# A head's sum of squares in the hgrn mixer: two rounded products instead of one plain F32 product

## What is computed

```python
proj = einsum('bsd,de->bse', h, w_in)
q, f_logit, i_val, g = split(proj, ...)
f = lb + (1.0 - lb) * sigmoid(f_logit)          # one decay for each token and key column
k = 1.0 - f
# in chunks of 64 tokens, 8 heads of 128 columns, state [128 keys, 128 values]:
o = (q * exp(b)) @ state + scores(q, k, b) @ v   # b: running sum of log f within the chunk
state = exp(b_last)[..., None] * state + (k * exp(b_last - b)).T @ v
...
o = rmsnorm(o, g_norm_w) * silu(g)               # over the 128 columns of each head
return einsum('bsd,de->bse', o, w_out)

def rmsnorm(x, g):
    return x * rsqrt(mean(x * x, axis=-1) + EPS) * g
```

## Time and profile before

| what | value |
|---|---|
| median of three runs | 2321.96 us (2321.89 to 2322.27) |
| profiled execution, span | 2320.9 us |
| instructions | 32131 |
| granted TensorE clock over the span | 1.000 |
| DMA, mean over the span | 98 GB/s, 226.30 MB |
| the hgrn head loop and its end | about 690 to 845 us of the span |
| TensorE busy in that stretch | 152.22 of 155.00 us |
| VectorE, ScalarE, GpSimd busy in it | 126.50, 130.46, 61.95 us |

### The profile page before, as it was taken

One profiled execution on the slowest core, in us unless ns is written; L12 is line 12 of the kernel. 1 busy time (PEld: TensorE's weight loads), 2 busy tenths in 40 slices (PEclk: granted clock), 3 DMA queues, 4 the chain that ended last, 5 costly groups with the idle time before them and its releaser, 6 DMA issues.

```text
span 2320.9 us, 32131 instructions
## 1 busy us (share of the span) xinstructions
PE 2309.1 (99%) x12088; PEld 1950.9 (84%) x12088; DVE 1498.3 (65%) x2173; ACT 1119.0 (48%) x1829; POOL 223.6 (10%) x313
## 2 busy tenths in 40 slices
PE   9999999999999999999999999999999999999999
PEld 8777889988888888999888778888888878888887
DVE  6665789952738968899428876777434456777731
ACT  6655544452539965445326854444323444544420
POOL 1221013200125410232000000000001000000000
PEclk9999999999999999999999999999999999999999
DMA  5433223332242222333322223323322323233232
GB/s 167 152 132 102 85 92 109 104 112 93 87 118 64 64 84 82 99 110 111 113 89 77 64 82 91 100 90 106 100 93 91 100 69 95 91 100 100 95 107 79
DMA packets 72541, 226.30 MB, mean 98 GB/s; under 512 B 7921, under 2 KB 19489, under 8 KB 72417
## 3 DMA queue, kind: packets, MB, share of 16 engines
q1 hardware_dynamic: 67840, 210.72, 28.5%
q0 software_dynamic: 4576, 13.89, 1.9%
HBM read 221.28 MB, written 2.18 MB: 96 GB/s over the span
## 4 chain that ended last, share of the span: by engine, by line
PE 92%; DVE 3%; ACT 3%; POOL 1%; issue 1%; DMA 0%; DVEq 0%; ACTq 0%; SPq 0%
PE bank L338 26%; PE bank L340 25%; PE bank L339 25%; PE bank L478 5%; PE bank L470 4%; PE bank L1605 1%; PE bank L1596 1%; PE bank L1639 1%; DVE w_lo L312 0%; DVE h L756 0%; POOL hgrn_lv L2560 0%; PE bank L2651 0%; PE bank L2015 0%; POOL hgrn_lv L2547 0%; PE bank L3103 0%
## 5 line engine op out<-in xcount | busy, mean ns | idle before, releaser
L312 DVE TENSOR_TENSOR w_lo<-raw,w_hi 128x1024 fp32r<-128x1024 f32 (+1 forms) x310 | 402.3, 1308 | 218.4 <-ACT w_hi L307 218.1
L338 PE MATMUL bank<-x_hi,w_hi 128*128 128x512 f32 x1344 | 529.2, 394 | 1.2 <-ACT sb_q L2761 1.0
L340 PE MATMUL bank<-x_hi,w_lo 128*128 128x512 f32 x1344 | 523.4, 389 | 0.0
L339 PE MATMUL bank<-x_lo,w_hi 128*128 128x512 f32 x1344 | 523.1, 389 | 0.0
L307 ACT ACTIVATE w_hi<-raw 128x1024 fp32r<-128x1024 f32 (+1 forms) x310 | 344.6, 1121 | 179.9 <-PE bank L340 93.5
L338 PEld LDWEIGHTS bank<-x_hi,w_hi 128*128 128x128 f32 x1344 | 252.3, 188 | 57.4 <-issue 3.1
L340 PEld LDWEIGHTS bank<-x_hi,w_lo 128*128 128x128 f32 x1344 | 252.2, 188 | 53.0
L339 PEld LDWEIGHTS bank<-x_lo,w_hi 128*128 128x128 f32 x1344 | 252.5, 188 | 51.2 <-issue 0.5
L338 PE MATMUL bank<-st_a_hi,w_hi 128*128 128x512 f32 (+1 forms) x396 | 145.1, 366 | 0.0
L340 PE MATMUL bank<-st_a_hi,w_lo 128*128 128x512 f32 (+1 forms) x396 | 144.7, 365 | 0.0
L1374 DVE TENSOR_TENSOR bank<-bank,rstd 128x512 f32<-128x512 f32 x120 | 83.2, 696 | 92.2 <-PE bank L340 92.2
(11 more groups left out here) (444 smaller groups left out, 4673.2 us busy)
## 6 DMA issues: line engine op xcount, KB each, us to landing
raw<-in_w_up SPq DMA_DIRECT2D x120, 512.0 KB, 3.5
raw<-in_w_down SPq DMA_DIRECT2D x64, 704.0 KB, 4.2
st_raw_even<-in_w_up SPq DMA_DIRECT2D x28, 512.0 KB, 4.2
st_raw_odd<-in_w_up SPq DMA_DIRECT2D x24, 512.0 KB, 4.0
raw<-in_w_fox_qk SPq DMA_DIRECT2D x16, 512.0 KB, 3.7
raw<-in_w_hgrn_qf SPq DMA_DIRECT2D x16, 512.0 KB, 3.5
fox_c_keys_a<-fox_c_rows POOLq DMA_DIRECT2D x8, 640.0 KB, 4.1
fox_c_keys_b<-fox_c_rows POOLq DMA_DIRECT2D x8, 640.0 KB, 4.5
```

The lines of the kernel that those rows point to most:

```text
L312: nc.vector.tensor_tensor(w_lo[:, slot, 0:size], raw[:, slot % 2, 0:size], w_hi[:, slot, 0:size].bitcast(F32), ALU.subtract).then_inc(sem( ...
L338: nc.tensor.matmul(out, w[0], x[0], start=first, stop=False)
L339: nc.tensor.matmul(out, w[0], x[1], start=False, stop=False)
L340: return nc.tensor.matmul(out, w[1], x[0], start=False, stop=last)
```

## The change

ScalarE squares bank 7 twice: into `ho` as plain F32, and into a new tile `square_hi` rounded to F32R. VectorE subtracts, `square_low = ho - square_hi`, also F32R (`square_rest`). TensorE multiplies both by rounded ones (`ones_r`) and adds them up in bank 5. `norm` waits for both squares ahead of the high product and for the subtraction ahead of the low one. `square_low` lies at the address of `ho`, so the subtraction is in place, and `square_hi` lies at the address of `hr`. `square_rest` stands between product 0 and product 1 in the loop, ahead of `near_take` in turn 8 and ahead of the weight conversion in turns 9 and 10. `hg_square_low` takes over the semaphore `fx_qk`.

```diff
-            "gla_min": ("fx_setup", 4), "gla_abs": ("fx_ls", 3),
+            "gla_min": ("fx_setup", 4), "gla_abs": ("fx_ls", 3), "hg_square_low": ("fx_qk", FOX_PAIRS),
...
         hg_masks_at = hg.at
+        at_ho = hg.at
         ho, hr = (hg.take(n, [P, T])[:] for n in ("ho", "hr"))
+        square_low, square_hi = (hg.take(n, [P, T], F32R, at=at_ho + 4 * T * i)[:] for i, n in enumerate(("square_low", "square_hi")))
...
             def norm(o):
 
-                wait(pe, "hg_sq", o + 1)
+                wait(pe, "hg_sq", 2 * o + 2)
                 wait(pe, "hg_st", 3 * o + 3)
-                nc.tensor.matmul(ps[5][:], ones[:], ho, start=True, stop=True).then_inc(sem("hg_ms"), 1)
+                nc.tensor.matmul(ps[5][:], ones_r[:], square_hi, start=True, stop=False)
+                wait(pe, "hg_square_low", o + 1)
+                nc.tensor.matmul(ps[5][:], ones_r[:], square_low, start=False, stop=True).then_inc(sem("hg_ms"), 1)
...
                         nc.scalar.activation(ho, ps[7][:], ACT.Square).then_inc(sem("hg_sq"), 1)
+                        nc.scalar.activation(square_hi, ps[7][:], ACT.Square).then_inc(sem("hg_sq"), 1)
...
+                def square_rest():
+                    if norm:
+                        wait(dve, "hg_sq", 2 * o + 2)
+                        tt_(square_low, ho, square_hi.bitcast(F32), ALU.subtract, "hg_square_low")
+
...
                 if proj:
                     product(0)
+                    square_rest()
                     product(1)
...
                 elif lev:
+                    square_rest()
                     near_take()
...
                 else:
+                    square_rest()
                     second_unit()
                     near_take()
```

## The result

The changed kernel takes 2325.89 us (median of 20 runs, 2324.93 to 2327.00) against 2322.31 us for the kernel before on the same chips (20 runs, 2321.53 to 2325.49): a ratio of 1.0015, interval 1.0009 to 1.0021, or +3.6 us (2.1 to 4.9). That lies inside the 0.2% that I had called no change, and on its slower side. The forecast was +2.2 us. The profiled execution happens to be the fastest of the 20. It spends 1.8 us outside its span, so its 2324.93 us are 2323.1 us of span, and that of before, 2320.9 us of span, stands for some 2322.7. (The 1.1 us named ahead of the prediction were the distance of that span from the median of three runs, and not the launch's ends, which are 1.8 us.) This pair alone shows +2.2 us, by luck the forecast; where the other 1.4 us come from had to be found out.

The account below looks back on a forecast made before the run. TensorE, 99% busy, was taken to set the pace, with ScalarE and VectorE close behind; 0.3 + 0.3 + 0.65 + 0.95 + 0 = +2.2 us, from 2321.96 to 2324.2 us, range 2321.0 to 2326.8 us.

Parts of the forecast that it names:

- TensorE saves 0.41 us a head: At each head's norm, two rounded products take 0.45 us in place of 0.86: 3.3 us less for eight heads.
- ScalarE +0.49 us, 0.15 left at kd: In the loop the second square costs ScalarE 0.49 us; waits cover part, leaving kd 0.15 us late, with 0.17 to spare.
- Low product, stall 0.24, pair 0.16 us earlier: In mid-loop TensorE stalls 0.24 us for the subtraction, so the pair gains 0.16 us in place of 0.41.
- State products wait for kd in every turn: In the loop kd is later by 0.15 us, so state products wait for ScalarE and start only 0.02 us earlier.
- Heads 2 to 4, +0.3: Mid-loop turns lose 0.10 us each, 0.12 for contention less 0.02 gained: +0.3 us (-0.15 to +1.4).
- the GpSimd rival: Subtraction's 0.60 us step delays GpSimd's level 2 difference, then kd: 0.43 us a head, total 2326.3 to 2328 us; 14%.
- Heads 0 and 1, +0.3: Early turns, where TensorE already waits, lose by ScalarE's 0.15 us lateness: together +0.3 us (0 to +0.9).
- Head 5, +0.65: At the tail the subtraction stands behind a weight conversion; TensorE stalls 1.5 us, VectorE wins back 0.45: +0.65 us (0.2 to 1.1).
- Head 6, +0.95: At the tail the subtraction comes after the takes, the pair ends at 830.42 against 829.46: +0.95 us (0.5 to 1.4).
- Head 7, 0: At the last head the low product waits about as long as the pair saves: 0 us (-0.4 to +0.3).
- Nothing behind the mixer takes it up: Behind the mixer TensorE has no gap to absorb the loss, so the +2.2 us goes to the end.
- the milder reading: VectorE's subtraction beside GpSimd: 0.12 us taken for contention, near the milder row, 0.61 us against 0.41; worst case 1.26.

Follow-up runs that it names:

- the second profile: The changed kernel as it is, profiled once more: 2326.19 us, with a span of 2324.4 us.
- the first: First profile of the changed kernel, the fastest of its 20 runs: 2324.93 us, with a span of 2323.1 us.
- the four profiles with a fallen clock: Variants of the changed kernel: pair in heads 0 to 4 only, 2323.58 us; subtraction earlier at the tail, 2325.82; norm later in the loop, 2326.48; both orders, 2325.43.

## Why the prediction was right, and where it was off

The direction, the class and the range (2321.0 to 2326.8) hold: 2325.89 us. Of the mechanism the larger half holds: TensorE's saving doesn't reach the end, and the tail is lost to a subtraction that stands behind other VectorE work. In mid-loop it holds for kd without the subtraction, but not with it: three of the signs that I gave didn't come (low product 0.4 to 0.6 us after the high one, near earlier, state products waiting for kd), and what the turn loses there it loses by the subtraction and GpSimd, which I had priced at 0.12 us. The size was 2.2 us for 3.6 measured. By its steps:

- **TensorE saves 0.41 us a head.** Confirmed where nothing waits: without the subtraction the pair takes 0.46 us from start to start instead of 0.86. By the page the busy time fell by 1.2 us only: with a stall in between, the page counts 0.40 us for the high product and 0.34 for the low one up to the next start, 0.74 against 0.86.
- **ScalarE +0.49 us, 0.15 left at kd.** Measured 0.49 and 0.11.
- **Low product, stall 0.24, pair 0.16 us earlier.** Wrong: counted as I did, from start to start, the stall is 0.71 - 0.23 = 0.48 us, twice the forecast (the bracket's 0.31 leaves out 0.17), and near starts 0.19 us later. The 0.12 us for contention was too little: the subtraction took 0.89 us, 0.21 more than 0.68, just what the row in its own place had shown (0.61 against 0.41 us), and GpSimd's difference grew by 0.27. Nor did I price that the matmul after the stalled one comes 0.34 instead of 0.23 us later.
- **State products wait for kd in every turn.** True without the low product's wait, not with it, where TensorE itself arrives later than kd.
- **Heads 2 to 4, +0.3.** Measured +0.60 and +0.49. It was the GpSimd rival in small: level 2 starts 0.27 to 0.29 us later against its turn, just short of the 0.3 from which I said it decides. The turn, 17.40 us in the second profile and 17.44 in the first, stands at the upper edge of the 17.1 to 17.4 that I gave, or just over it.
- **Heads 0 and 1, +0.3.** -0.05 with the race won, +0.61 with it lost, and in the four profiles with a fallen clock 0.2 to 0.5 us more (34.65 to 34.93 us from head 0's state products to head 2's, against 34.45). The term was sized from one profiled execution, and of the terms inside the mixer it is the one that varies most.
- **Head 5, +0.65.** Measured +1.0. The stall was right (1.58 us for 1.5), the 0.45 us to be won back weren't: the product did fall from 1.26 to 0.41 us, but VectorE waits 0.60 us for ScalarE's exponential (819.47), and ScalarE had waited 0.84 us for the turn of kd (818.32), which stands behind TensorE's stall. The second square, for which I had nothing at the tail, costs 0.6 us there by itself. **Head 6, +0.95:** 1.10. **Head 7, 0:** 0.1.
- **Nothing behind the mixer takes it up.** In both profiles 0.4 us are taken back at the norm that follows the mixer. In starts, TensorE is 2.53 us behind ahead of it; its wait for sum_lo, 0.5 us before, is gone, which leaves 1.77; and the wait for x_hi, 0.8 instead of 0.4, makes it 2.12. That the change is the cause isn't shown: the kernel with the plain product at the tail takes back 0.6 us at the same place.

The sum of these is +3.0 us for the second profile, in which the clock stayed at 1.00; with the 0.2 to 0.5 us of a fallen clock it is 3.2 to 3.5 of the 3.6 us measured, and the rest is within the interval. How often the clock falls in the 20 runs is not known. What stays open, too, is why some executions enter the mixer later than others, before any instruction that was changed: from 0.3 us earlier to 2.4 us later than the profile of before.

## What to carry to other kernels

A shorter list for the busiest engine is worth little when the chain that feeds it is as long: here kd, through ScalarE and GpSimd, was 0.2 us from being awaited. Take the work that the change gives them, not the work it takes from TensorE, as the first term. A wait that appears in front of the new instruction is not yet its cost; remove it and look whether the turn gets shorter, and if the next wait takes its place, the chain behind both is what to shorten. The cost also hangs on where the new instruction stands in its engine's queue, so place it before costing it: here three heads at the tail lost twice what five in the loop did.

## What the runs showed of the hardware

- **VectorE and GpSimd, one runs and the other waits.** With both starting within 0.01 us, the one took its usual time (the 310 of w_lo have a median of 1.23) and the other nearly the sum: w_lo 1.23 and GpSimd 2.12 us, or GpSimd 1.04 and w_lo 2.12 us, in two executions of the same kernel. The Trainium skill, "SBUF — State Buffer", "SBUF: two separate sides", says that the pair of ports they share is an exclusive lock, held by the one that starts first for its whole instruction while the other is blocked fully. The trace agrees on the lock: the loser's 2.12 us is 0.15 us short of 1.04 + 1.23. On who gets it the records can't tell: w_lo is recorded 0.01 us ahead in both executions (718.37 and 718.38, 719.01 and 719.02) and lost the first. I had used the milder reading, a stretch of 0.12 us.
- **It was shifted, not saved.** With the bank as its input VectorE's instruction left GpSimd's difference at 0.54 us instead of 1.17, and another product of VectorE took 1.26 us.
- **The clock after idle time.** With 1.6 and 0.5 us of idle time at head 0 the granted clock fell to 0.60 to 0.78 over 734 to 738 us in four profiles, and stayed at 1.00 in a fifth with the same waits (1.63 and 0.54 us). The three kernels that had the first wait (1.6 us) but none for the low product kept 1.00.
- **A rounded product after a wait** is followed by the next matmul 0.34 us later instead of 0.23, in the loop and at both stalls of the tail (817.35 to 817.69). The wait isn't the only occasion: the first product of a projection unit behind the transposes, with no wait, is followed 0.31 us later (768.02 to 768.33).
